# Two heads at a time in the first attention of a two-layer trunk, its values in 512-column chunks and three of its eight weight squares in seven products

## The reference, cut to what matters

```python
def diff_attention(h, w_qkv, q_gain, k_gain, lam, subln_g, w_o, rel_bias, layer_idx):
    qkv = h @ w_qkv                                  # (256, 2048) @ (2048, 6144)
    q, k, v = jnp.split(qkv, [nqk, 2 * nqk], axis=-1)
    q = rmsnorm(q.reshape(B, S, N_HEADS, 2, HEAD_DIM), q_gain)    # 8 heads, 2 maps, 128
    k = rmsnorm(k.reshape(B, S, N_HEADS, 2, HEAD_DIM), k_gain)
    v = v.reshape(B, S, N_HEADS, V_DIM)                           # 256 a head
    ...                                              # for each block of 128 queries:
        logits = einsum('bqhme,bkhme->bhmqk', qb, k) * scale + bias[:, None]
        p = softmax(where(dist >= 0, logits, NEG))
        a = p[:, :, 0] - lam_full * p[:, :, 1]       # the difference of two maps
        o = einsum('bhqk,bkhe->bqhe', a, v)
    o = rmsnorm(o, subln_g) * (1.0 - lam_init)
    return o.reshape(B, S, ATTN_WIDTH) @ w_o
```

## Time and profile before

| | us |
|---|---|
| median of 3 runs | 2496.64 (2495.29 to 2497.62) |
| span of the profiled execution | 2494.1 |
| PE busy in it | 2487.8 |
| DVE, ACT busy | 2100.0, 1464.0 |
| first attention with its start, 0 to about 357 us: DVE, ACT busy | 227.6, 191.8 |

### The profile page before, as it was taken

One profiled execution on the slowest core, in us unless ns is written; L12 is line 12 of the kernel. 1 busy time (PEld: TensorE's weight loads), 2 busy tenths in 40 slices (PEclk: granted clock), 3 DMA queues, 4 the chain that ended last, 5 costly groups with the idle time before them and its releaser, 6 DMA issues.

```text
span 2494.1 us, 30623 instructions
## 1 busy us (share of the span) xinstructions
PE 2487.8 (100%) x11823; PEld 2088.7 (84%) x11823; DVE 2100.0 (84%) x2387; ACT 1464.0 (59%) x1561; POOL 44.3 (2%) x54
## 2 busy tenths in 40 slices
PE   9999999999999999999999999999999999999999
PEld 8988888888888888888888888888888888888887
DVE  6656666999999999998778878776699999999998
ACT  5545555766767566556545545545566676766654
POOL 1000000000000000000000000000000000000000
PEclk9999999999999999999999999999999999999999
DMA  8554554757667557476556666654476666755754
GB/s 283 180 164 162 177 198 139 247 192 248 207 214 225 193 187 244 169 227 196 157 161 188 188 190 195 185 164 152 149 251 204 220 221 206 234 186 200 240 174 159
DMA packets 364820, 491.16 MB, mean 197 GB/s; under 512 B 19285, under 2 KB 216101, under 8 KB 362256
## 3 DMA queue, kind: packets, MB, share of 16 engines
q1 hardware_dynamic: 360448, 465.64, 56.5%
q0 software_dynamic: 4000, 23.63, 4.3%
q10 hardware_dynamic: 240, 0.10, 0.0%
HBM read 468.31 MB, written 3.68 MB: 189 GB/s over the span
## 4 chain that ended last, share of the span: by engine, by line
PE 98%; DVE 1%; ACT 0%; DMA 0%; issue 0%; ACTq 0%
PE psum L1945 43%; PE psum L1949 22%; PE psum L1831 8%; PE psum L1832 8%; PE psum L1838 8%; PE psum L2048 2%; PE psum L1958 1%; PE psum L1957 1%; PE psum L1956 1%; PE psum L2175 1%; PE psum L1787 0%; PE psum L2139 0%; PE psum L2173 0%; PE psum L2147 0%; PE psum L2159 0%; DVE w_lo L1116 0%
## 5 line engine op out<-in xcount | busy, mean ns | idle before, releaser
L1945 PE MATMUL psum<-w_hi,xT 128*128 128x512 f32 x3936 | 984.7, 390 | 0.0
L666 ACT ACTIVATE w_hi<-w_raw 128x2048 fp32r<-128x2048 f32 (+1 forms) x350 | 631.5, 1810 | 397.3 <-PE psum L1949 262.8
L1945 PEld LDWEIGHTS psum<-w_hi,xT 128*128 128x128 f32 x3936 | 736.6, 188 | 151.8
L1116 DVE TENSOR_TENSOR w_lo<-w_raw,w_hi 128x2048 fp32r<-128x2048 f32 (+1 forms) x332 | 705.3, 2145 | 55.7 <-ACT w_hi L666 55.4
L1949 PE MATMUL psum<-w_lo,xT 128*128 128x512 f32 x1968 | 516.0, 389 | 0.1
L1949 PEld LDWEIGHTS psum<-w_lo,xT 128*128 128x128 f32 x1968 | 369.3, 188 | 77.5 <-DVE w_lo L1116 1.0
L1831 PE MATMUL psum<-w_hi,xT 128*128 128x512 f32 (+1 forms) x1008 | 362.0, 369 | 0.0
L1832 PE MATMUL psum<-w_hi,xT 128*128 128x512 f32 (+1 forms) x1008 | 355.9, 363 | 0.0
L1124 DVE TENSOR_TENSOR w_lo<-w_raw,w_hi 128x2048 fp32r<-128x2048 f32 (+1 forms) x118 | 255.7, 2179 | 41.0 <-ACT w_hi L679 40.6
L679 ACT ACTIVATE w_hi<-w_raw 128x2048 fp32r<-128x2048 f32 (+1 forms) x118 | 215.3, 1830 | 102.7 <-PE psum L1949 63.1
L1945 PE MATMUL psum<-w_hi,mixT 128*128 128x512 f32 x896 | 239.6, 389 | 0.0
(11 more groups left out here) (201 smaller groups left out, 1919.1 us busy)
## 6 DMA issues: line engine op xcount, KB each, us to landing
w_raw<-in_f_w_up SPq DMA_DIRECT2D x352, 512.0 KB, 5.1
w_raw<-in_f_w_down SPq DMA_DIRECT2D x176, 512.0 KB, 5.1
w_raw<-in_b_w_qkv SPq DMA_DIRECT2D x192, 256.0 KB, 3.9
w_raw<-in_a_w_qkv SPq DMA_DIRECT2D x94, 512.0 KB, 4.4
w_raw<-in_b_w_qkv SPq DMA_DIRECT2D x256, 128.0 KB, 2.6
w_lo<-w_raw POOLq DMA_DIRECT2D x18, 1024.0 KB, 7.0
w_raw<-in_a_w_o SPq DMA_DIRECT2D x16, 1024.0 KB, 5.1
w_raw<-in_b_w_qkv SPq DMA_DIRECT2D x32, 512.0 KB, 6.2
```

The lines of the kernel that those rows point to most:

```text
L666: nc.scalar.activation(w_hi[:, slot, cols], w_raw[:, slot, cols], ACT.Copy).then_inc(hi_ready, 1)
L1116: nc.vector.tensor_tensor(w_lo[:, slot, cols], w_raw[:, slot, cols], w_hi[:, slot, cols], ALU.subtract).then_inc(lo_ready, 1)
L1945: pe.matmul(o, x[:, h, P * m:P * (m + 1)], hi, start=start and h == 0, stop=False)
```

## The change

Attention A goes by pairs of heads, in the same form as attention B. A pair has 15 chunks (entries e = 0 to 14): four of values for both heads (512 columns), then `THREE`: eight squares of queries and keys, of which numbers 4, 5 and 6 are a "one" followed by its "sum". The products of a pair alternate between PSUM banks 0 to 3 and 4 to 7 ("own"), and the fast squares also write the other four. The attention work of pair p - 1 stands between the entries of pair p and uses those other four banks too. The hardware loops are gone; the pairs are written out.

```diff
+A_ENTRIES = tuple(("all", j) for j in range(4)) + THREE
-A_STEPS = (0, 2, 3, 6)
-A_LAST_STEPS = (0, 2, 3, 5)
+A_STEPS = (2, 3, 5, 6, 8)
+A_LAST_STEPS = (1, 2, 4, 4, 5)
 # ACT, attention work of pair p after its share of the splits of entry j
+                if j == 0:
+                    a_squares(p)
                 if j == steps[0]:
+                    a_take_q(p, base)
                 if j == steps[1]:
+                    a_exp(p)
                 if j == steps[2]:
+                    a_take_aT(p, base)
                 if j == steps[3]:
+                    a_square_o(p, base)
+                    a_norm_o(p, base)
+                if j == steps[4]:
+                    a_take_oT(p, base)
 # DVE
+                if j == 0:
+                    a_norm(p)
+                if j == steps[0]:
+                    a_take_k(p, base)
+                if j == steps[1]:
+                    a_softmax(p, base)
+                if j == steps[1] + 1:
+                    a_subtract(p)
+                if j == steps[3]:
+                    dve.wait_ge(a_osq_ready, p + 1)
+                    rsqrt(o_r, o_ss, o_t, [(slice(0, 4), 1.0 / VD)], a_o_rstd)
+                if j == steps[4]:
+                    dve.wait_ge(a_to, p + 1)
+                    nc.vector.tensor_scalar(a_oT[:, 4 * p + 1:4 * p + 4:2, :], ...)
+            def a_pair(c, p, odd):                       # DVE
+                for e in range(A_PAIR):
+                    if e == 3:
+                        a_take_v(c + e, p, odd)
+                    if e + LEAD + 1 == A_ONES[0]:
+                        add_weights(c + A_ONES[0], c + A_SUMS[0])
+                    if p > 0 or e > 0:
+                        split_ahead(c, e, AO0)
+                    for one, to in zip(A_ONES[1:], A_SUMS[1:]):
+                        if e + LEAD + 2 == one:
+                            add_weights(c + one, c + to)
+                    if p == 0:
+                        begin(0, G_MIX, e)
+                        if e == 2:
+                            take_consts()
+                            mix_x(0)
+                        if e == 3:
+                            make_lambda()
+                            mix_low(0)
+                    else:
+                        a_attend(e, p - 1, A_STEPS, 4 - 4 * odd)
+            def a_pair(c, p, odd):                       # PE
+                    if e == 0:
+                        at_least(pe, a_p6_out, p)
+                    if e == 4:
+                        at_least(pe, a_combined, p)
+                    if e == A_SUMS[0] and p > 0:
+                        pe.wait_ge(a_oT_act, p)
+                        pe.wait_ge(a_oT_dve, p)
+                    a_entry_of(c + e, e, p, odd)
```

More of the change, by code:

```diff
@@ L145, in loads_of @@
     if A0 <= c < AO0:
-        return 2 if (c - A0) % A_HEAD < 4 else 1
+        return {"all": 1, "sum": 0}.get(kind(c), 4)
     if B0 <= c < BO0:
@@ L469, in load_x, with free_slot, load_a_pair @@
                 sp.dma_start(resid[:, :, cols], src).then_inc(x_in[q], 16)
-            def free_slot(c, more=None):
-                if more is None:
-                    lo_made(sp, c - SLOTS)
-                else:
-                    at_least(sp, lo_ready, c - SLOTS + 1 + more)
-            def load_a_head(c, h, more=0):
-                for j in range(A_HEAD):
-                    first = isinstance(h, int) and j < 4
+            def free_slot(c):
+                lo_made(sp, c - SLOTS)
+            def load_a_pair(c, p):
+                for e, (what, j) in enumerate(A_ENTRIES):
+                    if what == "sum":
+                        continue
+                    first = p == 0 and e < 4
@@ new lines, in a_entry_of, with high_made, low_made, lower_free @@
+            def a_entry_of(c, e, p, odd):
+                what, j = A_ENTRIES[e]
+                own, other = a_bank(odd), a_bank(1 - odd)
+                if what == "all":
+                    if p == 0 and e < 2:
+                        first_chunk(c)
+                    else:
+                        moving(c, range(4 * j, 4 * j + 4), 512, [(own, own + 1)], j == 0, j == 3)
+                    return
+                def high_made():
+                    pe.wait_ge(hi_ready, c + 1)
+                def low_made():
+                    lo_made(pe, c)
+                x = [xT[:, 2 * j + i, :, :] for i in range(2)]
+                if what == "std" and j == 0:
+                    def lower_free():
+                        pe.wait_ge(a_v_act, p + 1)
+                        pe.wait_ge(a_v_dve, p + 1)
+                    low_made()
+                    upper_first(c, x, own, lower_free)
+                elif what == "std":
+                    plain_square(c, x, own, False, 2 * j + 2 == KB, high_made, low_made)
+                else:
+                    i = MIXED.index(j)
+                    mix = [mixT[:, s, i, :, :] for s in range(4)]
+                    (fast_one if what == "one" else fast_sum)(c, x, mix, own, other, i == 0, i == len(MIXED) - 1,
+                                                              high_made, low_made)
```

706 lines of the change are left out of this document (331 added, 375 removed).

## The result

The changed kernel takes 2547.28 us (median of 4 runs, 2546.48 to 2550.29); the kernel before took 2495.97 (2495.16 to 2497.62) beside it. The ratio is 1.0209, 95% interval 1.0194 to 1.0223: 2.1% slower. Forecast: 2533, range 2512 to 2550; so it lies in the range, 3 us under its upper end, and the slowdown is 51 us where 36 were forecast. The profiled spans are 2545.9 and 2494.1: 51.8 us more.

What follows compares the result with a forecast made beforehand. PE was taken as the bound, busy 2487.8 of 2494.1 us. Waits of 43.7, PE's work of -14.0 and slow pace of 6.6 gave +36.3 on 2496.6, so 2532.9 us; range 2512 to 2550.

Steps and rivals of the forecast that it cites:

- First waits: After entry 5 in pairs 1 to 3, PE's transposes wait 3.0 us each for DVE's differences, which stand behind a split.
- Second waits: Before entry 9 in pairs 1 to 3, PE waits 6.2 us each for DVE's copy of the turned output.
- Out-projection: With the last pair's attention, PE's waits of 0.6, 1.4, 3.8, 0.9, 0.4 and 5.0 us sum to 12.1.
- First pair: After entry 3, PE waits 4.0 us for DVE's copy of the values, behind input root, constants and sums; bounds 0 and 8.
- PE's work: Attention: values save 4.8 us, queries and keys 8.2, and fewer blocks 1.0; 14.0 us off PE in all.
- PE's pace after it stood: Slow matmuls after four stops over 4.5 us cost 1.65 us each, 6.6 in all; bounds 0 and 15.
- The signs: Expected in the profile: the named PE waits, about 81 us between pairs 1 and 2, matmuls at 0.2275 us elsewhere.
- Sum: Whole kernel: waits 43.7 us, PE's work -14.0, slow pace 6.6; together +36.3 us.
- the pace stays: Rival: waits as forecast, but no slow matmuls after PE's stops; 2526 us, chance 0.30.
- the gain stands: Rival: the chains fit in PE's cover, so only the 14.0 us saved count; 2483 us, chance 0.05.
- the rival with the long chains: Rival: contention makes each chain a quarter longer, so waits grow from 43.7 to about 70 us; 2559 us, chance 0.09.
- DVE becomes the bound: Rival: DVE's work in a pair limits the kernel; counted at 61 of 72 us; no chance under this name.

Runs made afterwards that it cites:

- e1: Changed kernel with DVE making the differences ahead of its split in entry 4 (pairs 1 to 3); 2534.05 us, 1.0153.
- e2: Changed kernel with DVE copying the turned output ahead of the weight sums in entry 8, still behind the splits; 2536.21 us, 1.0161.
- e10: Changed kernel with, on PE alone, six matmuls of entry 9's sum moved ahead of the wait for the turned output; 2541.44 us, 1.0183.
- e7: Changed kernel, first pair only: DVE takes the constants before the input's root and makes the input's sums after the values' copy; 2542.38 us, 1.0184.
- e11: e9 with the sum's adds, squares, roots and first-pair constants ahead of splits, and one output split moved from entry 11 to 14; 2499.62 us, 1.0013.
- e5: Changed kernel with eight plain squares of queries and keys per pair, without the seven products and their weight sums; 2534.7 us, 1.0156.
- e4: Changed kernel with 24 useless matmuls of 512 columns on PE ahead of the second wait of pairs 1 to 3; 2541.9 us, 1.0185.
- e9: Changed kernel with steps reordered in pairs, first pair and out-projection, plus combination and out-projection roots ahead of splits, six sum matmuls ahead of PE's wait; 2501.8 us, 1.0024.
- e12: e11 with eight useless matmuls of 512 columns ahead of PE's wait in the out-projection's chunk 6; 2497.76 us, 1.0004.

## Why the prediction was right, and by how much

The direction and the mechanism were right. One size, the clock's, was off by 13 us, PE's saving by 3.5, both to the same side; the range held with 3 us to spare, since the rest came out nearly as counted.

- **First waits: right.** 3.0 forecast; 3.01 three times, for the DVE line that writes the differences. e1 removes them.
- **Second waits: right.** 6.2 forecast, 6.03 to 6.04 three times (the second of them below). The name was not: the profile says "issue", where I expected DVE's copy. e2 and e10 show that it is that copy.
- **Out-projection: right in sum.** 0.6, 1.4, 3.8, 0.9, 0.4, 5.0 forecast (12.1); 1.0, 1.6, 3.7, 0.9, under 0.2 and 5.1 measured (12.3). The 1.6 is partly luck: the 16 squares took 1.5 us more than in the chain that gave 1.4 (342.18 to 348.35 in ACT's timeline), and the split at its head began about 1 us before that chain's start.
- **First pair: the place right, the reason not.** 4.0 forecast for the copy of the values; 5.4 measured, for the constants that stand ahead of it on DVE (e7). By the prediction's own chain the constants are copied at 39.85 and PE is at their wait at 36.03, which is 3.8: that PE waits for them at entry 4 was overlooked. The rest of the 5.4 is mostly the load that came late, which it had put at nothing.
- **PE's work: 14.0 forecast, about 10.5 measured.** A pair was to need 72.0 us. In e11 the pairs come 72.77 apart with 0.30 of wait: 72.5, against 75.3 for two heads before. Over four pairs that is 11. Some 2 us of what is missing lies with the seven products, by e5; the other terms were not tried one by one.
- **PE's pace after it stood: the step that was mis-sized.** The prediction took the first small matmuls of the program as the measure, 22 x 0.075 = 1.65 us for each of four stops, and bounded it by 15. It was 19.6. Eight of the nine stops of 3.0 us and more brought the low clock, and it stayed for 3.0 to 6.3 us of busy time with every matmul at nearly double its price: 1.5 to 3.2 us lost at each. The forecast gave it to four stops, and its bound supposed that only so many matmuls are slow as at the program's start, each losing 0.075 us. Behind the stops all matmuls in the stretch are slow, large ones too, and one of 512 columns loses 0.2 us. The six transposes behind two first waits show the difference that the clock makes, at 1.00 in pair 1 and at 0.50 in pair 2; below them is the second of the 6.0 us waits:

```profile
124.77 0.87 PE L1880 MATMUL psum<-ident,phase 128*128 128x128 f32 x6 [3.01 <-DVE phase L1333]
...
208.95 1.54 PE L1880 MATMUL psum<-ident,phase 128*128 128x128 f32 x6 [3.01 <-DVE phase L1333]
...
233.84 0.77 PE L1977 MATMUL psum<-w_hi,mixT 128*128 128x512 f32 x1 [6.04 <-issue]
```

- **The signs.** A pair was to come 81 us behind the one before it; it came 85.7 (148.16 to 233.84). Matmuls were to keep 0.2275 elsewhere; behind eight stops they did not.
- **Sum.** 43.7 - 14.0 + 6.6 = 36.3 forecast; 43.4 - 10.5 + 19.6 = 52.5 by the rows, 51.8 measured in the spans and 51.3 in the medians.

The Trainium skill, "TensorE: Matmul & The Clock Gate", Part 1, says that the throttled clock is the default and activity releases it. The trace agrees, in the granted clock too (0.50 behind the stops), which the trace of before could not show, since PE hardly stood in it. The rival "the pace stays" (2526) is refuted by the granted clock and by e4, and "the gain stands" (2483) by the waits themselves; e11 shows the latter's mechanism, once the copies and differences do come ahead of the splits. By the time alone the rival with the long chains (2559) is as near to 2547 as the forecast; it is the waits that refute it, some 45 us and not 70. "DVE becomes the bound" is refuted in the pairs by e11, though DVE's work there has grown. The windows of one pair's length, before:

```profile
154.00:228.00 74.00, 74.00 (x434) 65.64 (x433) 45.51 (x71) 38.18 (x86) 0.00 (x0) 1.00 0.50 164
```

and in e11:

```profile
154.00:228.00 74.00, 73.70 (x344) 60.89 (x343) 61.01 (x80) 43.67 (x81) 0.00 (x0) 1.00 0.54 177
```

DVE is busy for 61 of 74 us (61 of 72 forecast), where it was 45.5. That is room enough for the work but not for a poor order: every step that DVE has in the chain to PE must stand ahead of the splits of chunks wanted later.

## What to carry to other kernels

When several small units of work are merged into a larger one, the serial chain between the engines gets longer while the cover between its steps stays; write down for each step when its input comes, what stands ahead of it in its engine's queue, and how much the waiting engine has left to do. On a kernel bound by PE, a stop can cost more than its length: here 45 us of stops cost 18 to 20 us more in clock. A saving of 0.4% in PE's work is worth having only if the order is redone with it, and even then it came out level here.

## What the runs showed of the hardware

- How long PE stood does not by itself say how much low clock follows. In the changed kernel the first stop of 3.01 us brought none, the two others 3.4 us of granted clock 0.50 each; in e4 two stops of the same 3.0 brought 6.8. A stop of 1.84 in e11 brought 3.4, one of 2.62 in e9 none. The stops of 6.0 brought 6.8 each time, two of 6.6 in e1 10.2 (the part of it in which PE stood included).
- The page's line of the clock in 40 slices hides this: it reads 9 in every slice of e12, which has two such stretches, since a slice is 62 us long:

```profile
PEclk9999999999999999999999999999999999999999
```

  It takes windows of a microsecond to see them.
- In the changed kernel a matmul of 512 columns takes 0.389 us in the record at the full clock and 0.632 at the low one, and starts 0.2275 and 0.427 us behind the one before; its weight load takes 0.188 and 0.334.
- A square with its sum on ACT (128 columns) costs 0.294 us with a fixed scale (kernel before) and 0.385 with one read from a tile (changed kernel).
